# Mixers: the fourth row tile ahead of the state's product, the state's product scaled ahead of the old states, half of y's heads one chunk later

## The reference, cut to what matters

```
# Mamba-2 part, per chunk of 128 tokens (cut)
y_diag = einsum(cb * decay, xdt)
states = einsum(bm, decay_end, xdt)
h      = h * chunk_decay + states            # carried state; h_prev is the state before the chunk
y_off  = einsum(cm, h_prev, exp(acs))
y      = (y_diag + y_off + x * d_skip) * silu(z);  y = rmsnorm(y) * gain
# mLSTM part (cut; the kernel runs it in chunks of 128)
num = einsum(qk_s, v) + s_inter * einsum(q, c_prev)
den = max(|sum(qk_s) + s_inter * einsum(q, n_prev)|, exp(-m_row))
h   = sigmoid(o) * num / den
mix = concat([y_A, y_B, y_C]) @ w_out
```

## Time and profile before

| what | value |
|---|---|
| median of three runs | 2961.27 us (2959.61 to 2961.4) |
| the profiled execution's own time | 2958.75 us |
| its span | 2956.7 us, so 2.05 us lie around it |
| TensorE busy | 2874.0 us, 97% of the span |
| VectorE busy | 1914.6 us, 65% |
| ScalarE busy | 1194.8 us, 40% |
| GpSimd busy | 385.2 us, 13% |
| granted TensorE clock, mean of the span | 0.991 of full speed |

### The profile page before, as it was taken

One profiled execution on the slowest core, in us unless ns is written; L12 is line 12 of the kernel. 1 busy time (PEld: TensorE's weight loads), 2 busy tenths in 40 slices (PEclk: granted clock), 3 DMA queues, 4 the chain that ended last, 5 costly groups with the idle time before them and its releaser, 6 DMA issues.

```text
span 2956.7 us, 36085 instructions
## 1 busy us (share of the span) xinstructions
PE 2874.0 (97%) x13608; PEld 2311.3 (78%) x13608; DVE 1914.6 (65%) x2608; ACT 1194.8 (40%) x2005; POOL 385.2 (13%) x496
## 2 busy tenths in 40 slices
PE   8999999999999889999999999999999999999998
PEld 4888888777777667777888778888888888888887
DVE  4768787766853348888433676766776666656656
ACT  5322222354443444554333533333533333545443
POOL 0000000012540126565112100000000000000000
PEclk9999999999999999999999999999999999999999
DMA  4222333445765767777779744444542223766863
GB/s 155 68 65 88 124 126 122 134 144 190 224 203 158 248 202 242 266 270 273 292 261 341 265 167 155 156 164 159 197 164 107 107 107 136 292 211 198 294 193 106
DMA packets 294569, 545.14 MB, mean 184 GB/s; under 512 B 59228, under 2 KB 150780, under 8 KB 284924
## 3 DMA queue, kind: packets, MB, share of 16 engines
q1 hardware_dynamic: 262636, 437.69, 44.4%
q0 software_dynamic: 24704, 75.52, 6.7%
q10 hardware_dynamic: 7056, 29.63, 2.6%
HBM read 358.30 MB, written 184.44 MB: 184 GB/s over the span
## 4 chain that ended last, share of the span: by engine, by line
PE 46%; DVE 2%; DMA 2%; ACT 1%; issue 0%; SPq 0%; DVEq 0%; ACTq 0%
PE f_banks L2864 25%; PE f_banks L2872 14%; PE f_banks L2045 6%; DMA f_h_raw<-hq 1%; DMA hq<-o_tq 1%; PE f_banks L2240 0%; DMA f_raw<-in_w_gu 0%; DVE f_w_op L2674 0%; DVE f_snap L2700 0%; DMA f_bop6lo<-hq 0%; DVE f_bop1lo L2667 0%; ACT o_late L2143 0%; ACT f_w_op L2549 0%; DVE f_a L2712 0%; DVE f_bop2lo L2667 0%
## 5 line engine op out<-in xcount | busy, mean ns | idle before, releaser
L2872 PE MATMUL f_banks<-f_d_op 128*128 128x512 f32 x1848 | 419.0, 389 | 0.0
L2872 PEld LDWEIGHTS f_banks<-f_d_op 128*128 128x128 f32 x1848 | 346.8, 188 | 72.0
L2738 DVE TENSOR_TENSOR f_d_op<-f_d_raw,f_d_op 128x1024 fp32r<-128x1024 f32 x154 | 187.5, 1225 | 148.9 <-ACT f_d_op L2581 148.2
L1861 PE MATMUL t_banks<-t_w_hi,h_hi 128*128 128x512 f32 (+1 forms) x640 | 249.5, 390 | 8.7 <-DVE t_w_lo L1722 8.5
L656 PE MATMUL t_banks<-h_hi,c_w_hi 128*128 128x512 f32 x640 | 255.8, 400 | 0.0
L656 PE MATMUL t_banks<-h_hi,c_w_lo 128*128 128x512 f32 x640 | 250.0, 391 | 0.0
L656 PE MATMUL t_banks<-h_lo,c_w_hi 128*128 128x512 f32 x640 | 249.1, 389 | 0.0
L2581 ACT ACTIVATE f_d_op<-f_d_raw 128x1024 fp32r<-128x1024 f32 x154 | 162.9, 1061 | 198.3 <-PE f_banks L2872 160.9
L1861 PE MATMUL t_banks<-t_w_lo,h_hi 128*128 128x512 f32 (+1 forms) x640 | 239.0, 373 | 0.0
L1861 PE MATMUL t_banks<-t_w_hi,h_lo 128*128 128x512 f32 (+1 forms) x640 | 238.4, 372 | 0.0
L2563 ACT ACTIVATE f_snap<-f_banks 128x1024 f32<-128x1024 f32 x88 | 90.3, 1026 | 258.6 <-PE f_banks L2864 258.6
(11 more groups left out here) (401 smaller groups left out, 6297.3 us busy)
## 6 DMA issues: line engine op xcount, KB each, us to landing
f_raw<-in_w_gu SPq DMA_DIRECT2D x88, 512.0 KB, 6.2
sop<-f_a SPq DMA_DIRECT2D x154, 256.0 KB, 2.0
f_d_raw<-sop SPq DMA_DIRECT2D x154, 256.0 KB, 2.8
t_raw<-in_w_tok SPq DMA_DIRECT2D x72, 512.0 KB, 4.6
f_d_raw<-top SPq DMA_DIRECT2D x88, 256.0 KB, 3.7
m_bc<-rows SPq DMA_DIRECT2D x16, 1152.0 KB, 6.8
f_d_raw<-in_w_dn SPq DMA_DIRECT2D x66, 256.0 KB, 3.1
o_y_lo<-y_lo SPq DMA_DIRECT2D x16, 1024.0 KB, 8.6
```

Of the source, the lines that this page charges most:

```text
L1861: last = nc.tensor.matmul(banks[:, t, 0:width], h[:, b, k_first + k, tok], w[unit % 2][at][:, cols], start=begins and k == 0 and j == 0, s ...
L2738: tt(d_op[d % D_RING][:, 2:4], d_raw[:, d % S_RING], d_op[d % D_RING][:, 0:2].bitcast(F32), sub).then_inc(dlo_ok, 1)
L2872: last = nc.tensor.matmul(banks[:, bank, :], d_op[d % D_RING][:, s, tok], d_op[d % D_RING][:, w, :], start=k == 0 and j == 0, stop=k == FU ...
```

## The change

Four things change, all in the mixers. The number of instructions and the work done are the same.

- TensorE: `project(c - 2, 3, 4)` (row tile 3, three matmuls) moves from behind the state's product to ahead of it, and so ahead of its wait for the gated scores.
- VectorE: `off` is computed before `h_old` and `c_old`, no longer after them.
- VectorE: of the six mLSTM heads of y of chunk c, only three are computed at the end of chunk c. The other three follow in chunk c + 1, right behind `off`. In the last chunk all six stay at the end.
- With that `y_ok` of chunk c comes in chunk c + 1, behind these three.

```diff
+        def rated(c, first, last):
+            for h in range(first, last):
+                e, i = h % 2, h // 2
+                at = slice(XW + h * DV, XW + (h + 1) * DV)
+                ins = stt(y[:, c % 2, at], num[:, e, i, 0:DV], den[:, 2, e, i:i + 1], zo[c % 2][:, at], mul, mul)
+                if h < HM - 1:
+                    chain(ins)
+                else:
+                    step(dve, ins, y_ok, c + 1)
...
-                chain(tt(h_old[:], h_state[:], decay[:, :, c:c + 1].to_broadcast([P, HS, HD]), mul))
-                chain(tt(c_old[:], c_state[:], decay_m[:, :, c:c + 1].to_broadcast([P, HP, DA]), mul))
-
                 dve.wait_ge(off_mm, c + 1)
                 if c >= 1:
                     dve.wait_ge(diag_read, c)
...
                 tt(o4, bank_x[:, :, 0:GW].rearrange("p g (h d) -> p g h d", h=HG), f4, mul).then_inc(off_read, 1)
+                if c >= 1:
+                    rated(c - 1, HM // 2, HM)
+                chain(tt(h_old[:], h_state[:], decay[:, :, c:c + 1].to_broadcast([P, HS, HD]), mul))
+                chain(tt(c_old[:], c_state[:], decay_m[:, :, c:c + 1].to_broadcast([P, HP, DA]), mul))
                 if c >= 1:
                     lower_y(c - 1, 0)
...
-                for h in range(HM):
...
+                rated(c, 0, HM // 2)
+                if c == TT - 1:
+                    rated(c, HM // 2, HM)
...
-                project(c - 2, 1, 3)
+                project(c - 2, 1, 4)
                 pe.wait_ge(gm_ok, 2 * c + 2)
...
                 last.then_inc(off_mm, 1)
-                project(c - 2, 3, 4)
                 transposes(c - 1, 0)
```

## The result

The changed kernel takes 3028.79 us (median of four, 3027.8 to 3030.36) against 2960.9 us for the kernel before on the same chip. The ratio is 1.0231, with a 95% interval of 1.0218 to 1.0244: slower by 68 us. The profiled execution took 3027.8 us, 69.0 more than that of before.

A forecast was written before the change was run, and what follows sets the result against it. TensorE, busy 97%, was taken as the bound. New stops (57.4 less 1.4), old stops gone (11.2 and 0.7) and clock (21 less 1.7) made +63.4 us, forecast 3024 us; 8 times in 10 within 2985 to 3052.

The forecast's parts named there:

- The new stop: TensorE ahead of the second group of transposes, waiting for the lower half: 4.1 us a chunk, 57.4 us in chunks 2 to 15.
- third rival: On the port shared with GpSimd, VectorE wins each time and GpSimd merely waits: 2951 us, chance 0.08.
- first rival: On VectorE only the heads wait for GpSimd, h_old and c_old do not: +47, 3008 us, chance 0.15.
- The whole instruction: Upper bound at the shared port: each of four VectorE waits lasts GpSimd's whole recorded instruction, 5.3 us, a stop of 5.4.
- 4.05 of waiting: Summed waits of heads 2 and 3, h_old and c_old on VectorE for GpSimd's instructions, in us a chunk.
- The clock: TensorE at half speed for about 3.4 us behind each new stop, costing 1.5 us a chunk, 21 us together.
- second rival: TensorE's granted clock does not fall behind the stops: +44, 3005 us, chance 0.13.
- the sum: Whole kernel: 57.4 - 1.4 - 11.2 - 0.7 + 21 - 1.7 = +63.4 us on the profiled execution.
- The old stop gone: TensorE's stop ahead of the state's product vanishes: 0.93 us in each of chunks 4 to 15, 11.2 us, and 0.7 in chunk 2.
- by this alone: TensorE's steady chunk, counting only scores 1.15 us earlier and 0.70 us more cover: 19.84 us a chunk.
- The load of zo: The next chunk's load, released later by y_ok, is hidden by the longer chunk and costs nothing.
- fourth rival: The load for the next chunk becomes the bound, at 21.2 us a chunk: +5, 2964 us, chance 0.04.

The follow-up runs named there:

- Experiment 1: Changed kernel with the word to GpSimd and TensorE that off is written given only behind c_old: 2953.86 us, ratio 0.9987.
- experiment 3: Changed kernel with h_old and c_old back ahead of off, row tile 3 and heads still moved: 2966.5 us, ratio 1.0030.
- experiment 2: Changed kernel with the diagonal product computed twice in chunks 2 to 15, as useless work in the stop: 3002.97 us, ratio 1.0150.
- Experiments 4: Kernel before with only row tile 3 moved ahead of the state's product: 2955.71 us, ratio 0.9990.
- 7: Changed kernel with c_old and the three late heads ahead of off, only h_old behind it: 2948.63 us, ratio 0.9964.
- 8: Changed kernel with the three late heads, h_old and c_old all ahead of off: 2954.89 us, ratio 0.9985.
- experiment 11: Kernel before with row tile 3 moved and GpSimd's second product (L1076) waiting for the last head of the chunk before: 2942.95 us, ratio 0.9941.
- experiment 6: Kernel before with only the three heads of y moved behind off: 2963.96 us, ratio 1.0017.
- experiment 5: Kernel before with only off moved ahead of h_old and c_old: 2951.11 us, ratio 0.9970.

## Why the prediction was right

**The new stop.** In the steady chunks each link came as written: off 1.49 us behind the state's product (1.60 said), head 1 ahead of GpSimd, the other two heads held up, h_old at 1.63 and c_old at 1.23, the lower half done at 9.7 and the transposes at 9.86 (9.98 said). Experiment 1 shows that GpSimd beside VectorE is the cause. The third rival (VectorE keeps the port) falls by the heads of 1.82 and 1.45 us. The first rival (only heads contend) falls by h_old and c_old themselves, and by experiment 3, where they are out of the way and the stop is 1.06. The Trainium skill (SBUF — State Buffer, "SBUF: two separate sides") had it that both would wait for the shared port pair; the trace after agrees, 1.63 for 0.95 us. "The whole instruction", taken literally, would have made the stop 5.4. Measured are 9.86 - 5.84 = 4.0 (3.96 of idle), and by its 0.35 us of own work head 3 began some 0.2 us before the recorded end of GpSimd's L1100: the handover comes before the recorded end. The working has a small slip: c_old's uncontended end of 5.28 and 4.05 of waiting make 9.33, not 9.21; measured is 8.98.

**The clock.** I took 1.5 us a chunk. It was about 2.0: 25.84 measured, less the mean of 23.82 of experiment 2, where the same loop runs at full clock. The second rival (no fall) is refuted by the granted clocks of 0.50 and 0.51 behind the stops, and experiment 2 gives the price: some 24 us, where the sum has 19.3. This mis-sized term is about the difference between 3024 and 3029. What the sum did not have is that the slow stretch is 6.8 us long half of the times; it stood there only as a bound.

**The first chunks, and some luck.** The stops made about 44 us, as the sum says, but not where it says. The steady chunks gave 0.2 us less each (23.82 - 20.80 = 3.02 in experiment 2, against 24.0 - 20.77 = 3.23). Chunk 1, which the sum leaves alone, got a stop of 5.32 us. The 3.30 of chunk 2 ahead of the state's product, which the sum mostly keeps, is gone: L1282 follows at 1129.68 without a stop. Chunks 1 and 2 together grew by 4.75 us (from 43.08 to 47.83) and not by 4.1 - 0.7 + 1.5 - 1.7 = 3.2.

**The old stop gone, and what it was worth.** The change does remove it, as said. But the account of the gain "by this alone" was wrong: that a chunk falls to 19.84 as soon as the scores come earlier. Experiments 4, 7 and 8 miss this. I had read the chain from the numerator to the scores as VectorE's own time, though in the kernel before its denominator (L1207, 0.94 us for 6 elements) was a wait for GpSimd in plain sight. It ends as GpSimd's L1076 ends:

```profile
1290.73 0.94 DVE L1207 SCALAR_TENSOR_TENSOR m_den<-m_num 128x6 f32<-128x6 f32 x1
```

```profile
1290.18 1.47 POOL L1076 TENSOR_TENSOR m_xskip<-m_tk,m_skip 128x768 f32<-128x768 f32 x1
```

The 19.84 us were measured behind chunk 2, where GpSimd had finished before the denominator came:

```profile
1145.75 0.17 DVE L1207 SCALAR_TENSOR_TENSOR m_den<-m_num 128x6 f32<-128x6 f32 x1
```

```profile
1143.76 1.47 POOL L1076 TENSOR_TENSOR m_xskip<-m_tk,m_skip 128x768 f32<-128x768 f32 x1
```

It did not hurt here, since the stop at the transposes hid it; the price of the third rival, 2951, rested on it. Experiment 1, which is that rival's world made real, has 20.51 a chunk, not 20.0.

**The load of zo** stayed hidden, as costed: there is no wait for it behind chunk 1. The fourth rival did not come to a test.

## What to carry to other kernels

Before an instruction is moved, look at what the other user of its port does at the new place. In these runs VectorE's instructions with two inputs in SBUF take turns with GpSimd's, one by one, and the short one pays a long one's time at each turn (0.35 us became 1.82). Those that read PSUM do not: the scores of 128x768 (L1168 in experiment 11) took 944 to 948 ns all 32 times, beside GpSimd and alone. A short instruction with a long duration (6 elements in 0.94 us, where 0.17 is enough) is a wait, and it can be the link through which an engine that is busy 13% of the time sets the pace. One line that makes that engine wait until its neighbour works from PSUM was worth as much here as the best reordering (0.9957 against 0.9964, within each other's intervals), and more together with the row tile (0.9941).

## What the runs showed of the hardware that was not expected

The length of a stop alone does not tell whether the clock falls. Stops of 1.06 us (experiment 3) were followed by 0.50 in three of the chunks, and stops of 0.95 (experiment 6) in two. Of the stops of 1.27 to 1.29 in experiment 2 only the one in chunk 2 was, and those of 0.78 never. In chunk 2 of the kernel before, a stop of 3.30 was followed by 0.50; in experiment 5 a stop of 3.32 at the same place was not:

```profile
1129.74 1.56 PE L1275 MATMUL t_side<-m_h,m_ch 128*128 128x384 f32 x4 [3.32 <-DVE m_bc L1161]
```

```profile
1129.80:1133.10 3.30, 3.30 (x15) 2.44 (x16) 3.30 (x4) 0.60 (x1) 0.67 (x1) 1.00 1.06 409
```

What decides between them was not tested and stays open.
